# One core, hybrid attention block: memory rows, transposes and products first, the first pair's queries between the last index units

## The reference

```
h     = rms_norm(x, g_in);  proj = h @ w_in          # split into qA kA vA qB kB vB qM gate qI kI wI
kM,vM = split(rms_norm(mem, g_mem) @ w_mem_kv)       # 4 heads of 64 each
oA    = dilated sliding-window attention, 8 heads
score = sum_h wI[t,h] * relu(qI[t,h] . kI[s])        # index scores, 8 heads, causal
oB    = attention over the 256 best-scored keys of each query, 4 heads
oM    = softmax(qM . kM) @ vM                        # 4 heads, over the 256 memory tokens
out   = rms_norm(x + (concat(oA,oB,oM) * silu(gate)) @ w_out, g_final)
```

## Time and profile before

| what | us |
|---|---|
| median of three runs (lowest, highest) | 707.63 (706.29, 709.75) |
| time of the profiled execution | 707.4 |
| its span | 705.6 |
| TensorE busy in the span | 672.8 |
| VectorE, ScalarE, GpSimd busy | 427.8, 333.1, 143.5 |

### The profile page before, as it was taken

One profiled execution on the slowest core, in us unless ns is written; L12 is line 12 of the kernel. 1 busy time (PEld: TensorE's weight loads), 2 busy tenths in 40 slices (PEclk: granted clock), 3 DMA queues, 4 the chain that ended last, 5 costly groups with the idle time before them and its releaser, 6 DMA issues.

```text
span 705.6 us, 11575 instructions
## 1 busy us (share of the span) xinstructions
PE 672.8 (95%) x4281; PEld 538.9 (76%) x4281; DVE 427.8 (61%) x991; ACT 333.1 (47%) x632; POOL 143.5 (20%) x95
## 2 busy tenths in 40 slices
PE   5999999999899999999999999989999999999993
PEld 4788887777678878787877788767788777777772
DVE  4857874396787579865896699462244364222247
ACT  6876653344335343634264435643663684221224
POOL 2021110111323011401311411410111165212101
PEclk9999999999999999999999999999999999999997
DMA  8521120111221132112111311110113227400005
GB/s 283 181 61 31 30 72 20 30 31 31 90 60 34 29 90 61 31 31 90 60 32 31 90 46 46 31 49 13 31 31 126 85 65 259 140 23 24 0 31 208
DMA packets 51863, 47.71 MB, mean 68 GB/s; under 512 B 5712, under 2 KB 44640, under 8 KB 51808
## 3 DMA queue, kind: packets, MB, share of 16 engines
q1 hardware_dynamic: 51808, 46.97, 21.5%
HBM read 39.62 MB, written 7.34 MB: 67 GB/s over the span
## 4 chain that ended last, share of the span: by engine, by line
PE 90%; DVE 3%; ACT 3%; issue 2%; DMA 1%; SPq 1%; DVEq 0%; ACTq 0%
PE j_ps L1506 30%; PE s_ps L1506 11%; PE o_ps L1665 8%; PE pt_ps L1639 8%; PE s_ps L1568 7%; PE s_ps L1714 5%; PE j_ps L1714 5%; PE o_ps L1506 4%; PE s_ps L1588 3%; PE pt_ps L1588 2%; PE s_ps L1685 1%; PE s_ps L1720 1%; PE j_ps L1720 1%; DMA gate<-in_w_in_dram 1%; PE o_ps L1482 1%
## 5 line engine op out<-in xcount | busy, mean ns | idle before, releaser
L1506 PE MATMUL j_ps<-h_hi,w_hl 128*128 128x512 f32 (+2 forms) x656 | 213.3, 391 | 4.2 <-DVE h_lo L1096 2.3
L1506 PEld LDWEIGHTS j_ps<-h_hi,w_hl 128*128 128x128 f32 (+1 forms) x656 | 121.1, 186 | 30.1 <-issue 4.4
L728 POOL TENSOR_TENSOR w_hl<-w_raw,w_hl 128x1024 fp32r<-128x1024 f32 (+1 forms) x29 | 68.3, 2355 | 316.0 <-ACT w_hl L830 290.6
L1506 PE MATMUL j_ps<-h_lo,w_hl 128*128 128x512 f32 (+2 forms) x328 | 125.3, 382 | 0.0
L1014 ACT ACTIVATE prob<-prob,nmax 128x256 f32<-128x256 f32 (+7 forms) x128 | 89.8, 703 | 36.4 <-DVE nmax L1310 26.5
L1002 ACT ACTIVATE probT<-pt_ps 128x512 f32<-128x512 f32 (+3 forms) x88 | 41.3, 470 | 130.5 <-PE pt_ps L1639 129.9
L1639 PE MATMUL pt_ps<-ident,prob 128*128 128x128 f32 x496 | 72.8, 280 | 3.1 <-ACT probT L1002 1.6
L1506 PE MATMUL s_ps<-h_hi,w_hl 128*128 128x512 f32 x224 | 74.4, 400 | 0.9 <-ACT qk L874 0.9
L1506 PEld LDWEIGHTS j_ps<-h_lo,w_hl 128*128 128x128 f32 (+1 forms) x328 | 61.1, 186 | 11.0
L1639 PEld LDWEIGHTS pt_ps<-ident,prob 128*128 128x128 f32 x496 | 55.2, 141 | 18.6 <-issue 12.2
L1237 DVE TENSOR_SCALAR_CACHE_REDUCE unread<-idx,tk 128x384 uint8<-128x384 f32 (+5 forms) x72 | 67.9, 942 | 1.4
(11 more groups left out here) (246 smaller groups left out, 1070.9 us busy)
## 6 DMA issues: line engine op xcount, KB each, us to landing
w_raw<-in_w_in_dram SPq DMA_DIRECT2D x27, 512.0 KB, 3.8
idx<-in_x_dram SPq DMA_DIRECT2D x8, 512.0 KB, 6.2
bias<-in_a_tab_dram SPq DMA_DIRECT2D x8, 512.0 KB, 4.4
mixed_scratch<-gate SPq DMA_DIRECT2D x12, 256.0 KB, 2.0
bias<-in_x_dram SPq DMA_DIRECT2D x4, 512.0 KB, 6.6
probT<-in_w_mem_kv_dram SPq DMA_DIRECT2D x4, 512.0 KB, 6.7
bias<-in_w_out_dram SPq DMA_DIRECT2D x4, 512.0 KB, 4.5
out_dram<-idx SPq DMA_DIRECT2D x4, 512.0 KB, 3.4
```

What stands on the lines that cost most here:

```text
L728: pool.tensor_tensor(w_hl[:, w % 2, 1, :, 0:n], raw_of(w)[:, :, 0:n], w_hl[:, w % 2, 0, :, 0:n].bitcast(F32), ALU.subtract).then_inc(w_lo_ ...
L1506: last = pe.matmul(bank[0:n, at:], a[:, k, 0:n], c[:, k, HALF * b + at:HALF * b + HALF], start=(k == 0 and q == 0), stop=(k == KD - 1 and ...
```

## The change

It moves the memory's work to the front of every engine's text.

- SyncE: memory rows, `wm` 0, rows 0 to 3 of `x`, `wm` 1 and 2, weights 0 and 1, rows 4 and 5, `wm` 3, rows 6 and 7, weight 2. `wm` 2 and 3 get buffers of their own in `prob[:, 0]`, so no load of them waits for a product; the unread squares go to `qk` and `linv`, the index weights' first half to `linv`.
- TensorE: `stay_busy(18)` in one piece, `turn_mem`, mem uses 0 and 1, then `turn_rows` of the first half, mem use 2, two `turn`, mem use 3, index keys first half, `turn_rows` of the second half, index queries 0 first half, two `turn`, memturn, and the two second halves and wturn.
- ScalarE and VectorE share `keep_mem` (four blocks each). The four rows of the first half get one chain in place of two.
- In the last group of index units the two uses of pair 0's queries stand in place of the mem uses, one k-step after each unit, four ahead of the first. Nothing is left between the last unit's k-step and the attention steps.

No product, transpose of data or copy is added or dropped; two `stay_busy` transposes fewer are made, and one root and one inverse chain.

```diff
--- before.py
+++ after.py
@@ -307,8 +307,8 @@
         else:
-            mine = [m for m, (kind, _, _) in enumerate(uses) if kind == "mem"]
-            head, each, kept = 8, 2, 0
+            mine = [m for m, (kind, w, _) in enumerate(uses) if kind == "w" and w == W_OF["q", 0]]
+            head, each, kept = 4, 1, 0
         units = list(range(PER_PAIR * j, PER_PAIR * (j + 1)))
@@ -376,9 +376,11 @@
         memT = v_sb[:, :, :, :].rearrange("p a b c -> p (a b c)").rearrange("p (k m) -> p k m", k=KD)
-        wm_raw = probT[:, :, :, :, :].rearrange("p a b c d -> p (a b c d)").rearrange("p (a k m) -> p a k m", a=2, k=KD)
+        wm_first = probT[:, :, :, :, :].rearrange("p a b c d -> p (a b c d)").rearrange("p (a k m) -> p a k m", a=2, k=KD)
+        wm_raw = [wm_first[:, w] for w in range(2)]
+        wm_raw += [prob[:, 0, w, :].rearrange("p (k m) -> p k m", k=KD) for w in range(2)]
         relu = [prob[:, 0, 0, :], prob[:, 0, 1, :], prob[:, 1, 0, :], prob[:, 1, 1, :]]
-        w_iT = [vT[0:H_I, :], v_b[0:H_I, :, :].rearrange("p t f -> p (t f)")]
+        w_iT = [linv[0:H_I, :, :, :].rearrange("p c a f -> p (c a f)"), v_b[0:H_I, :, :].rearrange("p t f -> p (t f)")]
         vmT = vT[:, 0:2 * N_MEM].rearrange("p (a m) -> p a m", a=2)
...
@@ -508,10 +511,10 @@
-        uses = [("w", w, b) for b in range(2) for w in range(2)] + [("wturn", 0, 0)]
+        uses = [("mem", w, 0) for w in range(4)]
+        uses += [("w", 0, 0), ("w", 1, 0), ("memturn", 0, 0), ("w", 0, 1), ("w", 1, 1), ("wturn", 0, 0)]
         uses += [("w", W_OF["qI", j], b) for j in range(1, PAIRS_I) for b in range(2)]
-        uses += [("mem", w, 0) for w in range(4)]
-        uses += [("w", W_OF["q", 0], 0), ("memturn", 0, 0), ("w", W_OF["q", 0], 1)]
+        uses += [("w", W_OF["q", 0], b) for b in range(2)]
         n_pre = len(uses)
@@ -588,27 +591,29 @@
             def load_wm(w):
-                if w >= 2:
-                    sp.wait_ge(j_done, use_number["mem", w - 2, 0] + 1)
-                sp.dma_start(wm_raw[:, w % 2], wm_k[:, :, P * w:P * w + P]).then_inc(wm_in[w % 2], 16)
+                sp.dma_start(wm_raw[w], wm_k[:, :, P * w:P * w + P]).then_inc(wm_in[w], 16)
...
             sp.dma_start(g_rows[KD:2 * KD, :], g_mem.rearrange("l (k p) -> (l k) p", p=P)).then_inc(rows_in, 16)
+            for r in range(NT, NT + MT):
+                load_rows(r)
+            load_wm(0)
             for r in range(NT // 2):
                 load_rows(r)
+            load_wm(1)
+            load_wm(2)
             load_w(0)
             load_w(1)
-            for r in range(NT // 2, NT + MT):
-                load_rows(r)
+            load_rows(4)
+            load_rows(5)
+            load_wm(3)
+            load_rows(6)
+            load_rows(7)
             load_w(2)
-            load_wm(0)
-            load_wm(1)
             sp.wait_ge(turned, 2 * KD)
...
                 load_w(w)
-            load_wm(2)
-            load_wm(3)
             next_w = PRE_W + 1
@@ -801,7 +806,7 @@
-            junk = prob[:, 0, 0, :]
+            junk = qk[:, 4, :]
             squares = [0]
@@ -884,7 +889,7 @@
                 last.then_inc(j_free, 1)
-                if m in key_uses and m > 0:
+                if m in key_uses and m != use_number["w", 0, 0]:
                     copy_keys(m)
@@ -899,10 +904,11 @@
+                act.wait_ge(g_ready, 1)
                 act.wait_ge(mem_turned, k // 2 + 1)
...
                 act.activation(memT[:, k, :], turn_banks[k // 2][:, cut], ACT.Copy,
-                               scale=g_cols[:, KD + k:KD + k + 1]).then_inc(mem_ready, 1)
+                               scale=g_cols[:, KD + k:KD + k + 1]).then_inc(mem_kept[0], 1)
@@ -910,37 +916,43 @@
+            first = use_number["w", 0, 0]
+            square_sum(NT)
+            root(NT, NT + MT)
+            act.wait_ge(x_inverse, 1)
+            act.activation(x_raw[NT + 1], x_raw[NT + 1], ACT.Copy, scale=stat[:, 3, NT + 1:NT + 2]).then_inc(mem_scaled, 1)
+            keep_mem(0)
+            keep_mem(1)
             square_sum(0)
+            keep_mem(4)
+            keep_mem(5)
             square_sum(2)
-            root(0, 3)
-            square_sum(3)
+            evacuate(0)
+            root(0, 4)
+            scale_row(2, 2)
             split_hi(0)
-            root(3, 4)
-            scale_row(2, 1)
+            evacuate(1)
             split_hi(1)
-            act.wait_ge(g_ready, 1)
             for v in range(KD):
                 high(v)
+            evacuate(2)
             square_sum(4)
...
             root(4, 8)
-            evacuate(0)
+            evacuate(3)
             scale_row(7, 3)
-            copy_keys(0)
+            evacuate(first)
+            copy_keys(first)
             for v in range(KD, 2 * KD):
                 high(v)
-            evacuate(1)
-            square_sum(NT)
-            square_sum(NT + 1)
-            root(NT, NT + MT)
-            evacuate(2)
+            evacuate(first + 1)
+            evacuate(first + 2)
+            evacuate(first + 3)
             split_hi(2)
-            evacuate(3)
-            for k in range(KD):
-                keep_mem(k)
+            evacuate(first + 4)
             split_hi(3)
-            evacuate(4)
+            evacuate(first + 5)
             for what, n, k in idx_schedule(uses):
@@ -953,13 +965,7 @@
                         split_hi(uses[n][1] + 2)
-            m = use_number["w", W_OF["q", 0], 0]
-            evacuate(m)
-            evacuate(m + 1)
-            evacuate(m + 2)
-            split_hi(PRE_W + 1)
-            m += 3
-            assert m == n_pre
+            m = n_pre
@@ -1097,7 +1103,7 @@
-            junk = prob[:, 0, 1, 0:HALF]
+            junk = linv[:, :, :, :].rearrange("p c a f -> p (c a f)")
@@ -1126,28 +1132,12 @@
-            def scale_rows(a, b, squared):
-
-                begin_chain(a, b, squared)
-                end_chain(a, b)
-                for r in range(a, b if a >= NT else b - 1):
-                    scale_row(r)
-
-            dve.wait_ge(g_turned, 1)
-            dve.tensor_copy(g_cols[:, :], o_ps[:, 0:2 * KD]).then_inc(g_ready, 1)
-            square_sum(1)
-            dve.wait_ge(g_ready, 1)
-            begin_chain(0, 3, 2)
-            end_chain(0, 3)
-            scale_row(0)
-            begin_chain(3, 4, 3)
-            scale_row(1)
-            end_chain(3, 4)
-            scale_row(3)
-            for v in range(KD):
-                low(v)
-            square_sum(7)
-            scale_rows(4, 8, 6)
+            def keep_mem(k):
+
+                dve.wait_ge(mem_turned, k // 2 + 1)
+                cut = slice(N_MEM * (k % 2), N_MEM * (k % 2) + N_MEM)
+                dve.tensor_scalar(memT[:, k, :], turn_banks[k // 2][:, cut], g_cols[:, KD + k:KD + k + 1], None,
+                                  ALU.mult).then_inc(mem_kept[1], 1)
@@ -1187,13 +1177,36 @@
+            dve.wait_ge(g_turned, 1)
+            dve.tensor_copy(g_cols[:, :], o_ps[:, 0:2 * KD]).then_inc(g_ready, 1)
+            square_sum(NT + 1)
+            dve.wait_ge(g_ready, 1)
+            begin_chain(NT, NT + MT, 1)
+            end_chain(NT, NT + MT)
+            dve.tensor_scalar(x_raw[NT], x_raw[NT], stat[:, 3, NT:NT + 1], None, ALU.mult).then_inc(mem_scaled, 1)
+            square_sum(1)
+            for k in (2, 3, 6, 7):
+                keep_mem(k)
+            square_sum(3)
+            begin_chain(0, 4, 3)
+            end_chain(0, 4)
+            for r in (0, 1, 3):
+                scale_row(r)
             split_low(0)
+            split_low(1)
+            for v in range(KD):
+                low(v)
+            square_sum(7)
+            begin_chain(4, 8, 6)
+            end_chain(4, 8)
+            for r in (4, 5, 6):
+                scale_row(r)
+            split_low(use_number["w", 0, 0])
             for v in range(KD, 2 * KD):
                 low(v)
-            split_low(1)
-            scale_rows(NT, NT + MT, 8)
-            split_low(2)
-            split_low(3)
+            split_low(use_number["w", 1, 0])
+            split_low(use_number["w", 0, 1])
+            split_low(use_number["w", 1, 1])
@@ -1216,8 +1229,6 @@
                                              op0=ALU.mult, op1=ALU.add).then_inc(idx_added, 1)
-            for b in range(2):
-                split_low(use_number["w", W_OF["q", 0], b])
             dve.wait_ge(idx_added, len(IDX_UNITS))
@@ -1459,8 +1470,7 @@
                 if n == 0:
-                    pe.wait_ge(x_ready, NT - 2 + MT)
-                    pe.wait_ge(lo_ready, 2 * KD)
+                    pe.wait_ge(mem_scaled, MT)
                 for a in range(2):
@@ -1476,10 +1486,10 @@
                     if ks[0] == 0:
-                        pe.wait_ge(wm_in[w % 2], 16 * (w // 2 + 1))
-                        pe.wait_ge(mem_ready, KD)
+                        pe.wait_ge(wm_in[w], 16)
                     for k in ks:
```

(46 more changed lines are left out.)

## The result

The change is slower. Median of 20 runs 709.8 us (707.76 to 712.18) against 707.71 (706.12 to 710.55) in 20 runs of the kernel before: ratio 1.0031, 95% interval 1.002 to 1.0042. That is 2.1 us, inside the range and inside "no difference over 0.5%", but it is a loss where a gain of 0.9 was forecast.

A forecast was written before the change was run, and what follows sets the result against it. TensorE, busy 95% of the span, was taken to bound the kernel, so only its idle time could move. 13.5 - 13.8 - 1.4 + 0.8 = -0.9 against the profiled 707.4 gave 706.5, median 706.7; range 704.5 to 710.0.

The forecast's parts named there:

- late transfers: Rival: queue pauses or slower `wm` loads make TensorE stand at mem use 1 or 3; +1.8, 709.5; chance 0.20.
- the clock case with 1.5 of slip: Rival: clock falls in the opening's wait for `o_ps`, +0.6, 708.2, chance 0.25; with 1.5 of slip, the range's end 710.0.
- The likeliest case: The forecast itself: whole kernel 0.9 us faster, median 706.7, no clock fall in the opening's wait; chance 0.40.
- moved copies cost nothing: Whole kernel: ScalarE and VectorE stay beside TensorE except where named, so moved copies add 0.
- The new wait: Opening, index keys' second half: TensorE idles 2.7 where it idled 1.1, until `o_ps` is evacuated and split, to 45.15.
- -13.8 - 1.4 + 0.8: Index units and end: four mem uses leave (-13.8), memturn's hole leaves (-1.4), the uncovered end adds 0.8.
- The term +0.8: Behind the last index unit: relu, add and split run in line without cover, 2.2 idle in place of 1.45.
- no fall in the new wait: Opening, wait for `o_ps`: the granted clock does not fall there, costing 0; the forecast case, chance 0.40.
- fills stand close on both sides: Argument against a clock fall in the opening's 2.7 us wait, beside an earlier 1.1 wait at 29.03 that caused none.
- signs of being wrong: TensorE waiting for `probT` or `prob`; clock below 1.00 between 12 and 60; VectorE's adds ending late-unit waits; first unit outside 57.5-61.
- hardly any transfer time is filled: Opening: it takes up 14.3 us of memory work and grows by 13.5, since new loads push old ones back.
- The clock rises late: Rival: transposes don't count for the clock, so memory transposes and half of mem use 0 run slow; 1.7 + 1.7, 710.1; chance 0.03.

The follow-up runs named there:

- the third experiment: Changed kernel with ScalarE splitting weight 3 behind the fourth index unit's relu, not ahead of the index weights' copy: 708.2 us, ratio 0.9998 to the kernel before.
- the first four experiments: Single edits of the changed kernel: memturn in another bank 0.9961, wait filled with throwaway transposes 1.0006, weight 3 split later 0.9998, two k-steps ahead 0.9991.
- the new end: Changed kernel with two k-steps of pair 0's queries ahead of the last group of index units in place of four: 707.85 us, ratio 0.9991.
- the three edits together: Changed kernel with memturn in another bank, weight 3 split later and two k-steps ahead of the last group: 702.59 us, ratio 0.9927.
- the second experiment: Changed kernel with 22 throwaway transposes filling TensorE's 2.5 us wait behind memturn: 708.09 us, ratio 1.0006 to the kernel before.
- the first experiment: Changed kernel with memturn using the bank of the index weights' transposes, so the index keys' second half needn't wait for `o_ps`: 705.31 us, ratio 0.9961.

## Why the prediction was wrong

The time was in the range, 0.2 below its upper end, and "no difference over 0.5%" (0.81) came true. The first was in part luck: the range's upper end stood for late transfers, and none was late, or for the clock case with 1.5 of slip that had no cause named, and it is this slip that came. The likeliest case had the wrong direction. Two terms of its sum failed: "moved copies cost nothing" (0 in place of 0.8), and the clock (0 in place of about 2). By its steps:

- **Transfers.** `gate` landed at 15.23 + 6.4 = 21.6 (said 21.8). TensorE waited for no transfer in the opening. Right.
- **The opening.** Mem uses ended at 16.3, 19.8, 25.9 and 30.2 (said 16.3, 19.7, 26 and 30.1). The new wait ended at 44.96 (said 45.15). Right, nearly to the tenth, because each term was a row and TensorE's order was the chain. The first unit started at 60.48 (said 59.05; the terms as listed, 45.15 + 11 + 1.2 + 1.39, give 58.74). Of the 1.4 between, 1.6 are the half clock.
- **The sentence that failed: "Moved copies cost nothing".** I asked when weight 2 is needed and not what stands behind weight 3's split on ScalarE. The load for that split is issued only when GpSimd has split weight 2, and ScalarE's part of weight 2's split had moved from 37.77 to 54.17, behind the index keys' second half, while the first unit moved by less, 14.95. Before, weight 3 landed just in time, while ScalarE made the memory copies. It cost 0.8 in the wait for `w_i`; with weight 3 split later the third experiment shows no such wait. From the first unit to the first fill of the attention steps TensorE took 83.20 before and 69.57 after, 13.6 less where -13.8 - 1.4 + 0.8 = -14.4 was forecast: the missing 0.8 is this wait.
- **The end.** From the last unit's end to the first fill it took 126.98 to 130.05 = 3.07 (said 3.15). The term +0.8 holds: the edit with two k-steps gave 0.9 back in the profile.
- **The whole in the profiles:** -0.9, + 0.8 for that wait, + 1.4 in the opening (1.6 of half clock, less 0.2 by which the new wait ended early), + 1.7 for the fall at 130.4 make 3.0 of the 3.1 between the spans.
- **The sum without the clock** becomes -0.9 + 0.8 = -0.1. The runs at like clock bear this out. Seventeen runs of the changed kernel had a mean granted clock of 0.990 or less and three had more; of the latter, two at 0.992 took 708.1 and 708.3, and four runs of the kernel before at 0.991 and 0.992 took 707.6 to 707.9. At 0.989 and 0.990 the changed kernel's nine runs mean 709.5, and 13 of the kernel before at 0.989 mean 710.0. At a given clock the two are the same within 0.5. (The 20 runs beside the changed kernel's have no clock on record, so these are the kernel before's 33 runs of the first four experiments.)
- **The clock: right mechanism, wrong weight.** I took "no fall in the new wait" as likeliest (0.40 against 0.25). The mean granted clock of the 20 runs is 0.9889, and of the 33 runs of the kernel before that came with the first four experiments 0.9918. The difference, 0.0029 x 708 = 2.1 us, is the size of the whole result. It follows the edits: 0.9888 to 0.9890 in the three kernels that have the idle wait and the old end (the changed one, weight 3 later, `wm` earlier), 0.9903 with the new end, 0.9910 and 0.9911 with the wait filled or gone, 0.9920 with the three edits together. Eight of the 20 stood at 0.987, with a mean of 711.1; of the 33 none did. One fall of 3.4 us at half clock is 3.4 x 0.5 / 708 = 0.0024 in the mean, so it is a little over one more fall in each execution. The argument "fills stand close on both sides" was no reason; the earlier trace rows had shown a fall behind 5.20 us in which TensorE was busy 3.54, and ahead of 45.1 it was busy 2.82 of 5.20. The rival itself was priced too low, at +0.6: it had one fall, in the wait, and neither the 0.8 nor a fall at the end of the units, a place that the prediction never named. Of its signs of being wrong one came, the granted clock below 1.00 between 12 and 60.
- **The claim that hardly any transfer time is filled** holds as it was made: 14.3 of memory work went in, and the first unit starts 14.95 later, 1.6 of it by the clock (7.31 against the 5.72 of the second experiment): about 1 us of idle time was filled.
- **The clock rises late.** This rival, by which transposes do not count for the clock, is out. The changed kernel's 18 throwaway transposes took 4.10, 0.23 each, and the memory's 16 behind them 1.99, 0.12 each, before TensorE had made one product. The 22 transposes of the second experiment kept the clock at 1.00. The Trainium skill, "TensorE: Matmul & The Clock Gate", section "Part 4: PE-mode transpose", says that the full clock does not engage for transposes, as they do not count as TensorE being busy; here the measurement decides. (The profile does not name the mode in which a transpose is issued.) The moment of the rise differs between executions: the 16 took 2.82 in the first experiment's. The granted clock reads 1.00 from the first microsecond in the profiles of the kernel before, of the changed one and of the first experiment, so this start shows in the pace alone and is not in the mean clocks above.

## What to carry to other kernels

When work is moved between an engine's stages, write down for each bank and each small load who stands behind it in the new order: the three costs here (a bank whose evacuation was queued behind eight copies, a split queued ahead of a copy that others needed, a relu with no cover) were all of that kind, and mended they turned +0.3% into -0.7%. A wait of 2.5 us on TensorE is to be priced at its length plus up to 1.7 for the clock (three of four profiles paid it here), unless throwaway transposes can stand in it. Where executions scatter in steps, compare the mean granted clock before the medians: it told here that the two kernels were equal within 0.5 at a like clock, and the edits then showed which idle time lowered it.

## What the runs showed of the hardware that I had not expected

- The same wait of 2.38 us was followed by 3.4 us at half clock in the changed kernel, in the run with two k-steps and in the run with `wm` loaded earlier, and not in the run with weight 3 split late.
- The kernel before, too, runs at three mean clocks: of 33 runs 13 at 0.989 (mean 710.0 us), four at 0.991 and 0.992 (707.7), 16 at 0.994 and 0.995 (707.2). Only one of the 20 runs of the changed kernel had more than 0.992.
- The clock's first rise is a matter of chance also: the 18 throwaway transposes took 4.10 in the changed kernel and the 16 behind them 1.99; with memturn's bank changed the same 18 took 4.10 and the 16 behind them 2.82.
